# First units of a down projection: one store for the conv rows, x1 in eight tiles behind later units, operand places in the order in which they come free

## The reference

```python
    x1 = _ln_affine(DN_ALPHA * x + gt_m * mix, lw['ln1_g'], lw['ln1_b'])
    h2 = _ln_plain(x1) * (1.0 + sc_f) + sh_f
    f_out, conv_new = _conv_ffn(h2, conv_buf, lw['w_up'], lw['w_gate'], lw['conv_w'], lw['conv_b'], lw['w_down'])
    x2 = _ln_affine(DN_ALPHA * x1 + gt_f * f_out, lw['ln2_g'], lw['ln2_b'])
```

## Time and profile before

| | |
|---|---|
| median of three runs | 2294.94 us (2292.55 to 2297.18) |
| profiled execution: time / span | 2294.87 / 2293.1 us |
| mean granted clock of TensorE | 0.97 |
| TensorE busy | 2129.7 us (93%) |
| VectorE / ScalarE / POOL busy | 1099.0 (48%) / 793.0 (35%) / 927.4 us (40%) |
| down projection on TensorE | 2026.2 to 2264.4 us |

### The profile page before, as it was taken

The page is one execution under the profiler, slowest core; times in us unless marked ns, Lnnn a source line. Parts: engine busy times, 40 slices in busy tenths (PEclk is TensorE's granted clock), DMA queues, the critical chain, the costliest instruction groups (busy, mean ns, idle before and its releaser), DMA issues. The chain is left out here.

```text
span 2293.1 us, 37946 instructions
## 1 busy us (share of the span) xinstructions
PE 2129.7 (93%) x15414; PEld 1880.0 (82%) x15414; DVE 1099.0 (48%) x1983; ACT 793.0 (35%) x1592; POOL 927.4 (40%) x637
## 2 busy tenths in 40 slices
PE   5998999999999999978999999999899999969995
PEld 3997788856777699977889998789899999958884
DVE  5114332255676710369420155667855455535538
ACT  3203222134665612346412322243333333324532
POOL 2322222111111132122311141563787877856777
PEclk9999999998999999998999999999999999989997
DMA  7564434283100052000321132222244434376751
GB/s 259 193 219 160 162 113 145 96 290 133 31 31 11 1 139 56 19 8 22 92 80 53 37 111 79 72 77 71 88 158 152 151 129 152 126 280 222 220 166 74
DMA packets 152725, 268.21 MB, mean 117 GB/s; under 512 B 17745, under 2 KB 86283, under 8 KB 147950
## 3 DMA queue, kind: packets, MB, share of 16 engines
q1 hardware_dynamic: 144343, 222.70, 29.4%
q0 software_dynamic: 8208, 43.07, 5.3%
HBM read 211.93 MB, written 58.08 MB: 118 GB/s over the span
## 5 line engine op out<-in xcount | busy, mean ns | idle before, releaser
L3445 PE MATMUL PS<-down_parts 128*128 128x512 f32 x924 | 213.1, 392 | 0.0
L3445 PEld LDWEIGHTS PS<-down_parts 128*128 128x128 f32 x924 | 173.6, 189 | 37.4 <-issue 1.2
L3402 PE MATMUL PS<-part_hi,w_ring 128*128 128x258 f32 x1152 | 191.5, 284 | 0.0
L3402 PE MATMUL PS<-sum_blocks,w_ring 128*128 128x258 f32 x1296 | 164.4, 286 | 13.9 <-DVE out_sums L3934 8.5
L3402 PEld LDWEIGHTS PS<-sum_blocks,w_ring 128*128 128x128 f32 x1296 | 160.2, 192 | 16.4 <-DVE out_sums L3934 10.8
L3402 PEld LDWEIGHTS PS<-part_hi,w_ring 128*128 128x128 f32 x1152 | 161.1, 190 | 4.3 <-issue 4.3
L3786 POOL TENSOR_TENSOR down_parts<-down_raw,down_parts 128x512 fp32r<-128x512 f32 x71 | 119.3, 1689 | 62.5 <-ACT down_parts L3600 62.3
L644 POOL TENSOR_TENSOR w_merge_parts<-w_merge_raw,w_merge_parts 128x1024 fp32r<-128x1024 f32 x24 | 59.6, 2506 | 201.9 <-ACT w_merge_parts L637 201.9
L2344 PE MATMUL PS<-h_hi,w_merge_parts 128*128 128x344 f32 x768 | 131.4, 323 | 0.0
L3600 ACT ACTIVATE down_parts<-down_raw 128x1024 fp32r<-128x1024 f32 x77 | 81.6, 1063 | 129.8 <-DMA down_raw<-w_down 57.3
L3736 POOL TENSOR_TENSOR w_ring<-w_raw,w_ring 128x512 fp32r<-128x512 f32 x72 | 102.6, 1425 | 56.3 <-ACT w_ring L3582 56.3
(11 more groups left out here) (596 smaller groups left out, 5175.3 us busy)
## 6 DMA issues: line engine op xcount, KB each, us to landing
down_raw<-act_blocks SPq DMA_DIRECT2D x77, 256.0 KB, 3.1
w_or_ada<-w_ada SPq DMA_DIRECT2D x8, 2048.0 KB, 10.4
w_raw<-w_up SPq DMA_DIRECT2D x11, 1024.0 KB, 9.5
w_raw<-w_gate SPq DMA_DIRECT2D x11, 1024.0 KB, 6.7
w_down_rows<-w_down SPq DMA_DIRECT2D x11, 1024.0 KB, 7.6
w_down_blocks<-w_down_sums SPq DMA_DIRECT2D x11, 1024.0 KB, 8.8
down_raw<-w_down_blocks SPq DMA_DIRECT2D x44, 256.0 KB, 3.6
act_blocks<-act_sums SPq DMA_DIRECT2D x10, 1024.0 KB, 5.2
```

The costliest lines, as they stand in the source:

```text
L3402: last = pe.matmul(out[:, c, :], r32(w[:, k, :]), r32(h[:, k, QUART * c:QUART * c + QUART]), start=first and k + i == 0, stop=k == 3 and i ...
L3445: last = pe.matmul(PS[:, t, :], r32(s[:, x, P * (t % 4):P * (t % 4) + P]), r32(s[:, y, :]), start=first and i == 0, stop=last_j and i == 2 ...
```

## The change

- **Conv rows.** The six groups go to one buffer in the memory of the down sums (`acc`, whose rows 4 to 7 are written first in a later pass), so that no copy waits for a store, and one store takes all, after unit 14's loads. TensorE transposes three groups after unit 1 and three after unit 5, in three banks, where it did one after each of units 1 to 6. ScalarE waits for this store before it writes that memory.
- **x1.** Eight loads of one token tile, 512 KB each, after the loads of units 15 to 22, in place of one of 4 MB before unit 8. dec_y moves from unit 16 to 23, g2 from 8 to 24, b2 from 8 to 26.
- **Places.** Units 6 to 8 take the memory of the weight ring and its sums, units 9 to 11 that of the activations and w_down rows. ScalarE's waits follow.
- **Sums of w_down.** POOL forms the last ones after unit 7, SyncE stores them after unit 9's loads.
- **VectorE** copies dec_row before unit 8's lower part (it was after unit 9's), the gate row before unit 10's; TensorE makes the gate transposes after unit 7 (was 4) and the spreading product after unit 9 (was 8).

```diff
-        slots = [low(f"down_parts{i}", [P, 4, 512], 16512 * (i // 2) + 8192 * (i % 2) if i < 6 else 49536 + 8192 * (i - 6))
-                 for i in range(12)]
+        slots = [low(f"down_parts{i}", [P, 4, 512], x) for i, x in enumerate(
+            [16512 * (i // 2) + 8192 * (i % 2) for i in range(6)] + [49536 + 8192 * i for i in (3, 4, 5, 0, 1, 2)])]
...
-        newR, lastR, gr = misc[32:32 + NB, :], rows3[0:2 * FT, 0:P], drow[0:NB + 1, :]
+        newR = acc[0:NB, 4:8, :, :].rearrange("p t h n -> p (t h n)")[:, 0:FF]
+        lastR, gr = rows3[0:2 * FT, 0:P], drow[0:NB + 1, :]
...
-            for w in (6, 7):
+            for w in range(6, NP * 7):
                 down_operands(w)
-            keep_down(NP - 1)
-            sp.wait_ge(mm_done, LAST_SUM)
-            sp.dma_start(xr[:, :, :], x1[0:L, :].rearrange("(t p) n -> p t n", p=P)).then_inc(x_in, 16)
-            for w in range(8, NP * 7):
-                down_operands(w)
-                if w == 8:
+                if w == 9:
+                    keep_down(NP - 1)
+                if w == 14:
+                    sp.wait_ge(new_read, 6)
+                    sp.dma_start(o["ffn_conv_s"][0, :, 1, :], newR).then_inc(new_out, 16)
+                    sp.wait_ge(last_read, 1)
+                    sp.dma_start(o["ffn_conv_p"][0, 0].rearrange("j (f p) -> (j f) p", p=P), lastR[:, :]).then_inc(new_stored, 16)
+                if 15 <= w < 15 + NT:
+                    t = w - 15
+                    sp.wait_ge(mm_done, LAST_SUM)
+                    sp.dma_start(xr[:, t, :], x1[P * t:P * t + P, :]).then_inc(x_in, 16)
+                if w == 23:
+                    sp.wait_ge(upd_done, NP)
+                    sp.dma_start(dec_y, x1[L:T, :]).then_inc(xd_in, 16)
+                if w == 24:
                     sp.wait_ge(wd_kept, 16 * NP)
                     sp.wait_ge(kept, 48 * NP)
                     sp.dma_start(g2[:, :], a["ln2_g"].to_broadcast([P, D])).then_inc(g2_in, 16)
+                if w == 26:
                     sp.dma_start(b2[:, :], a["ln2_b"].to_broadcast([P, D])).then_inc(b2_in, 16)
-                if 8 <= w < 14:
-                    n = w - 8
-                    f = min(FT, 4 * n + 4) - 4 * n
-                    sp.wait_ge(new_read, n + 1)
-                    sp.dma_start(o["ffn_conv_s"][0, :, 1, 512 * n:512 * n + P * f], newR[:, 512 * (n % 2):512 * (n % 2) + P * f]).then_inc(new_out[n % 2], 16)
...
+                if w in (1, 5):
+                    if w == 5:
+                        pe.wait_ge(new_read, 3)
+                        pe.transpose(PS[0:2 * FT, 6, 384:512], upl[:, :, :].rearrange("p j f -> p (j f)"), ident[:, :]).then_inc(tr_last, 1)
+                    else:
+                        pe.wait_ge(upd_done, NP)
+                    for n in range(3 * (w // 5), 3 * (w // 5) + 3):
+                        for f in range(4 * n, min(FT, 4 * n + 4)):
+                            last = pe.transpose(PS[0:NB, 4 + n % 3, P * (f % 4):P * (f % 4) + P], upd[:, f, :], ident[:, :])
+                        last.then_inc(tr_new, 1)
+                if w == 7:
+                    pe.wait_ge(new_read, 5)
...
-                    if w < 8:
+                    act.wait_ge(cv_done, 4 * NP)
+                    if w in (9, 10):
                         act.wait_ge(kept, 48 * NP)
                         act.wait_ge(actd_done, NP)
-                    if w in (7, 8):
+                    if w in (10, 11):
                         act.wait_ge(dec_done, FT)
                         act.wait_ge(wd_sums, 4 * NP)
-                    if w >= 10:
-                        act.wait_ge(cv_done, 4 * NP)
...
-                if w == 5:
+                if w == 7:
                     down_sums(NP - 1)
...
-                if n >= 2:
-                    v.wait_ge(new_out[n % 2], 16 * (n // 2))
-                v.tensor_copy(newR[:, 512 * (n % 2):512 * (n % 2) + cols], PS[0:NB, CONV, 0:cols]).then_inc(new_read, 1)
+                v.tensor_copy(newR[:, 512 * n:512 * n + cols], PS[0:NB, 4 + n % 3, 0:cols]).then_inc(new_read, 1)
...
+            for n in range(3):
+                new_rows(n)
+            down_low(6)
+            down_low(7)
+            v.wait_ge(dec_done, FT)
+            v.wait_ge(wd_kept, 16 * NP)
+            for q in range(4):
+                v.tensor_copy(dec_row[:, DQ * q:DQ * q + DQ], PS[32 * q:32 * q + NB, DEC_BANK, 0:DQ]).then_inc(dec_read, 1)
+            down_low(8)
+            for n in range(3, 6):
+                new_rows(n)
```

More of the change, by code:

```diff
@@ L3149, in ffn @@
         p_in = [sem(f"fd_p_in{i}") for i in range(4)]
-        new_out = [sem(f"fd_new_out{i}") for i in range(2)]
+        new_out = sem("fd_new_out")
         new_stored, stored = sem("fu_stored"), [sem("fd_stored0"), sem("fd_stored1")]
@@ L3347, in _ @@
             sp.wait_ge(new_stored, 32)
-            for s in range(2):
-                sp.wait_ge(new_out[s], 48)
+            sp.wait_ge(new_out, 16)
             sp.wait_ge(stored[0], 16 * (NT // 2 + 1))
@@ L3483, in _ @@
                     pe.wait_ge(new_read, 6)
+                    pe.wait_ge(last_read, 1)
                     pe.wait_ge(dec_read, 4)
@@ L3672, in copies @@
             def copies(p):
+                if p == D5:
+                    act.wait_ge(new_out, 16)
                 for t in range(4):
@@ L3989, in residual @@
                 v.wait_ge(gated, count)
-                v.wait_ge(x_in, 16)
+                v.wait_ge(x_in, 16 * NT)
                 residuals(v.scalar_tensor_tensor(y, y, ALPHA, acc[:, t, half, :], ALU.mult, ALU.add))
             v.wait_ge(upd_done, NP)
-            new_rows(0)
-            v.wait_ge(tr_last, 1)
[L3996 to L4004, removed]
+            for n in range(3):
[9 more added lines that the diff above has]
+                new_rows(n)
+            v.wait_ge(tr_last, 1)
+            v.tensor_copy(lastR, PS[0:2 * FT, 6, 384:512]).then_inc(last_read, 1)
+            down_low(9)
             v.wait_ge(gr_mm, 1)
             v.tensor_copy(gr, PS[0:NB + 1, 4:6, :].rearrange("p a n -> p (a n)")).then_inc(gr_read, 1)
[L4007 to L4010, removed]
             down_low(10)
-            new_rows(5)
             down_low(11)
```

## The result

The changed kernel takes 2281.32 us (median of five runs, 2275.18 to 2282.40), the kernel before 2293.33 us (five runs, 2292.55 to 2297.18). The ratio, taken from all five runs on either side, is 0.9938, with a 95% interval of 0.9923 to 0.9954: 14 us less, between 11 and 18 (the two medians are 12.0 us apart). Forecast were 2279.8 us in a range of 2276.5 to 2284.0.

A forecast was written before the change was run, and what follows sets the result against it. TensorE was taken to be held after unit 4 by a conv-row store and unit 8's loads, both behind x1's 4 MB. 21.3 - 4.1 - 2.1 = 15.1 us less: 2294.87 - 15.1 = 2279.8 us, range 2276.5 to 2284.

The forecast's parts named there:

- the stop and its clock: TensorE's idle time after unit 4, 19.2 us, plus slow clock afterwards, 2.1 us: 21.3 us to be saved.
- The stop: New TensorE wait before the gate transposes, for conv copy 4 behind the stored w_down sums: 4.1 us added.
- The clock: Work after the new stop runs at half clock for about 4.2 us, half of it lost: 2.1 us added.
- The bounds of the stop for POOL's pace: Length of the new stop with faster or slower POOL lower parts and sums: 3.3 to 4.9 us.
- The gate product with unit 12's lower part behind it: Gate matmuls moved after unit 9, VectorE waiting with unit 12's lower part queued: hidden, margin 1.5 us, cost nothing.
- The places: New memory places of units 6 to 8 delay no split that TensorE needs: cost nothing.
- the lead of 6.7 us: Unit 16 ready at 2077, wanted by TensorE at 2083.7; carries the x1 tiles, staying above 4 us: cost nothing.
- the first: Rival: the clock holds or the new stop is shorter, giving 2276.9 or 2277.7 us (2273.6 without the wait); chance 0.14.
- The store didn't land late: Rival: w_down sums' store lands late or POOL is slower; stop 5 to 7.6 us, 2280.7 to 2283.3; chance 0.20.
- A fixed time per tile standing in the queue: Rival: each x1 tile holds the queue 2.05 us extra; 12.9 us given back, 2292.7 us; chance 0.03.
- Unit and tile one after the other: Rival: unit loads and x1 tiles alternate, 6.95 us a unit; 24.1 us given back, 2303.9 us; chance 0.03.
- no other wait held TensorE between 2042 and 2060: Rival: some other wait, such as the conv store's new place, holds TensorE there; about 2291 us; chance 0.02.

The follow-up runs named there:

- two of the kernels without a stop: Changed kernel with VectorE's dec_row copies back behind unit 9's lower part (0.9920), or with POOL's last sums back after unit 5 (0.9919); each 245.6 us from unit 0.
- the other profile: The changed kernel measured once more, unaltered: 253.4 us from unit 0 to the end, ratio 0.9921.
- the best kernels: Changed kernel with dec_row copies later (0.9920), sums earlier (0.9919), sums earlier and old places (0.9910); kernel before with one conv-row store and x1 tiles (0.9924).

## Why the prediction was right

**What is removed.** 21.3 us were expected, from the stop and its clock. Both are gone, and two of the kernels without a stop are at 245.6 us: 266.9 - 245.6 = 21.3 us less. That the two causes had to go together was in the text ("the store that blocks VectorE and the 4 MB in front of unit 8"), but not their shares; by the runs, either one removed alone leaves a stop of 11 us.

**What is added.** Step by step, with 4.36 us added to the times after: ScalarE's split of unit 6 at 2037.5 (forecast 2037.42); POOL's sums start at 2042.1 (2041.5), since its two lower parts took 3.50 us and not 3.0; they end at 2047.3 (2046.9) after 5.26 us; the store landed after 5.01 us (5.19), at 2052.4 (2052.1); VectorE's second conv copy is there at about 2056.2 (2056.1); TensorE arrives at 2051.9 (2052.0). The stop: 4.37 us (4.1). The clock: 1.62 (2.1), and 2.68 in the other profile. The sum: 15.3 us in one profile and 13.5 in the other (266.9 - 253.4), 15.1 forecast; the ratio says 14. The mechanism came as forecast, step by step. That the first profile meets the sum within 0.2 us is partly luck: its stop was 0.3 us longer and its clock 0.5 us cheaper than forecast, and the second profile has both dearer. The bounds of the stop for POOL's pace were added up wrongly: 3.3 comes out as 3.5 and 4.9 as 4.6, which changes nothing in the forecast. The estimate by the fit of the Trainium skill ("DMA: Bandwidth & Descriptors", Anatomy of one DMA), 4.4 us for the megabyte, is under both rows, 5.19 and 5.01 us; the rows decide.

**What was costed at nothing.** The gate product with unit 12's lower part behind it: no stop there, but it was nearer than forecast. VectorE ended that lower part at 2067.03, after 1.66 us beside POOL's work on unit 15 where 0.95 was forecast, and TensorE wanted it at 2061.90 + 5.70 = 2067.6: a margin of 0.6 us and not 1.5. The places: nothing, as the run with the old ones shows. x1's tiles: no stop; the lead of 6.7 us was mis-sized, it is 5.0. The same late lower part makes 0.7 of that, and the landing, the split with its subtraction, and TensorE's own arrival 0.3 to 0.4 each. That it would shrink by 0.7 over the tiles was close (0.4 from unit 16 to 21).

**The rivals.** The clock did fall, so the first is out. The store didn't land late. A fixed time per tile standing in the queue is out: 390 GB/s at a share of 1.02 while the tiles go through, and the one transfer of 4 MB costs 6.8 us more where there is no cover. The rule of the Trainium skill ("DMA: Bandwidth & Descriptors", Bandwidth) to batch transfers to 1 MiB or more speaks of the transfer's own rate. Here the time that a transfer holds others back decides. Unit and tile one after the other: out by the same rows. And no other wait held TensorE between 2042 and 2060, so the change did what it says.

## What to carry to other kernels

Where an engine stands for long, two waits may end almost together, and the trace names the last; ask for each what is left when the other goes: alone these saved 7.4 and 8.8 us, both together 20.2. When work that waits for a transfer is put ahead of work that others wait for, write down when the transfer is issued, not when it was before: one moved block (the sums) and one moved wait (dec_row) were harmless alone and cost 6 to 8 us together. And a change that looks worthless next to a stop must be tried again once the stop is gone.

## What the runs showed of the hardware

- The price of the clock after a stop isn't a constant, and the stop's length doesn't set it. For stops of 3.6 to 19 us it was 1.60 to 2.85 us, with no order in it: 2.10 after 19.19 us, 1.60 after 10.95, 2.85 after 4.52. Two executions of the same kernel gave 1.62 and 2.68 after stops of 4.37 and 4.70.
- What sets it is how long the clock stays at half once TensorE works again; half of that time is lost, in all eight profiles within 0.2 us. In the first execution TensorE worked at half clock from about 2052.8 to 2056.2, in the second from 2057.67 to about 2063.2. In these eight, all with a stop of 3.6 us or more, the clock fell 2.7 to 5.3 us after TensorE had stopped, so that a stop can end before the fall and still be paid for. A stop of 0.74 us cost nothing.
- One store of 1 MB with no bulk transfer ahead of it took 5.19 us before, 5.01 and 5.02 in the two profiles of the changed kernel, 5.01 with the whole x1 after unit 15 and 4.93 with the x1 tiles alone; by such a row a wait could be forecast to some tenths of a us. Behind the 4 MB it took 7.65.
- The start of unit 0 varied by 9 us between executions of code that is the same up to there, against effects of 2 to 6 us. What makes it vary was not looked into, and the ratios of the best kernels (0.9910 to 0.9924) don't tell them apart from the changed one's second measurement (0.9921); that they are 6 to 8 us faster rests on the intervals of the profiles.
